# Seven block products for eight in the output and down projections of a two-block transformer kernel

## The reference

```python
xn = rms_norm(h, mix_norm[l])
proj = jnp.einsum("bsd,dp->bsp", xn, w_in[l]) + b_in[l]
...
merged = (jax.nn.sigmoid(ga) * jnp.einsum("bsc,cd->bsd", attn, w_attn_branch[l])
          + jax.nn.sigmoid(gc) * jnp.einsum("bsc,cd->bsd", conv, w_conv_branch[l]))
h = h + jnp.einsum("bsd,de->bse", merged, w_out[l])
hn = rms_norm(h, ffn_norm[l])
up = causal_depthwise_conv(jnp.einsum("bsd,df->bsf", hn, w_up[l]), ffn_conv_w[l])
gate, val = jnp.split(up, 2, axis=-1)
h = h + jnp.einsum("bsf,fd->bsd", jax.nn.silu(gate) * val, w_down[l])
return rms_norm(h, final_norm)
```

## Time and profile before

| | |
|---|---|
| median of 3 runs | 1052.56 us (1052.18 to 1054.4) |
| span of the profiled execution | 1050.5 us, 2.1 below the median |
| TensorE busy | 1038.4 us, 99% of the span |
| VectorE busy | 593.9 us, 57% |
| ScalarE busy | 445.9 us, 42% |
| GpSimd busy | 51.0 us, 5% |
| weight loads by SP, 512 KB each | 150, 3.5 us from issue to landing |

### The profile page before, as it was taken

How to read it: one execution, slowest core, us unless ns; L and a number is a source line. 1 busy time by engine, 2 the same in 40 slices (tenths; PEclk the granted TensorE clock), 3 DMA queues, 4 the chain that set the end, 5 groups by cost and what they waited for, 6 DMA issues and landing times.

```text
span 1050.5 us, 13952 instructions
## 1 busy us (share of the span) xinstructions
PE 1038.4 (99%) x5453; PEld 846.1 (81%) x5453; DVE 593.9 (57%) x1110; ACT 445.9 (42%) x855; POOL 51.0 (5%) x71
## 2 busy tenths in 40 slices
PE   9999999999999999999999999999999999999997
PEld 7877778888888888888888888899888677777785
DVE  6466665445356666533466563553456673567757
ACT  5355542233345434431234442453244454556640
POOL 0000000000001100000000000125200001000000
PEclk9999999999999999999999999999999999999999
DMA  7421133222341842333122323334211222511012
GB/s 277 160 65 57 61 101 100 95 89 98 123 140 41 275 152 87 98 125 110 61 101 85 100 97 110 131 122 135 91 61 61 61 81 71 211 41 41 21 61 80
DMA packets 29106, 107.08 MB, mean 102 GB/s; under 512 B 3227, under 2 KB 3371, under 8 KB 28401
## 3 DMA queue, kind: packets, MB, share of 16 engines
q1 hardware_dynamic: 24864, 86.13, 24.8%
q0 software_dynamic: 4032, 19.96, 5.3%
q10 hardware_dynamic: 144, 0.10, 0.0%
HBM read 101.44 MB, written 7.36 MB: 104 GB/s over the span
## 4 chain that ended last, share of the span: by engine, by line
PE 88%; DVE 5%; ACT 4%; issue 2%; DMA 2%; DVEq 0%; SPq 0%; ACTq 0%
PE ps L780 26%; PE ps L782 25%; PE ps L781 25%; PE ps L1054 2%; PE ps L1222 2%; PE ps L1205 1%; PE ps L1187 1%; DMA raw<-wp 1%; ACT whi L1285 1%; PE ps L1143 1%; PE ps L1106 1%; ACT SC L1336 1%; PE ps L1175 1%; DVE wlo L1633 0%; DVE SC L1739 0%
## 5 line engine op out<-in xcount | busy, mean ns | idle before, releaser
L780 PE MATMUL ps<-XH,whi 128*128 128x512 f32 (+1 forms) x864 | 336.7, 390 | 0.6 <-DVE XL L1646 0.2
L782 PE MATMUL ps<-XH,wlo 128*128 128x512 f32 (+1 forms) x864 | 326.9, 378 | 0.0
L781 PE MATMUL ps<-XL,whi 128*128 128x512 f32 (+1 forms) x864 | 326.5, 378 | 0.0
L1633 DVE TENSOR_TENSOR wlo<-raw,whi 128x1024 fp32r<-128x1024 f32 (+1 forms) x158 | 191.6, 1218 | 166.7 <-ACT whi L1285 166.1
L1285 ACT CAST whi<-raw 128x1024 fp32r<-128x1024 f32 (+1 forms) x158 | 161.2, 1027 | 95.9 <-PE ps L782 70.5
L780 PEld LDWEIGHTS ps<-XH,whi 128*128 128x128 f32 x864 | 162.6, 188 | 43.0 <-issue 12.4
L782 PEld LDWEIGHTS ps<-XH,wlo 128*128 128x128 f32 x864 | 162.6, 188 | 31.2
L781 PEld LDWEIGHTS ps<-XL,whi 128*128 128x128 f32 x864 | 162.8, 188 | 27.8 <-issue 0.5
L780 PE MATMUL ps<-whi,GH 128*128 128x512 f32 x176 | 68.8, 391 | 0.0
L782 PE MATMUL ps<-whi,GL 128*128 128x512 f32 x176 | 68.5, 389 | 0.0
L781 PE MATMUL ps<-wlo,GH 128*128 128x512 f32 x176 | 68.5, 389 | 0.0
(11 more groups left out here) (305 smaller groups left out, 1333.1 us busy)
## 6 DMA issues: line engine op xcount, KB each, us to landing
raw<-wp SPq DMA_DIRECT2D x150, 512.0 KB, 3.5
vec_dram<-row_dram POOLq DMA_DIRECT2D x1, 3072.0 KB, 13.7
H<-x POOLq DMA_DIRECT2D x1, 2048.0 KB, 8.1
x_dram<-H POOLq DMA_DIRECT2D x1, 2048.0 KB, 8.8
A<-w1c POOLq DMA_DIRECT2D x2, 1024.0 KB, 6.3
A<-x_dram POOLq DMA_DIRECT2D x1, 2048.0 KB, 12.8
y<-A SPq DMA_DIRECT2D x8, 256.0 KB, 2.0
raw<-wp SPq DMA_DIRECT2D x4, 402.0 KB, 3.9
```

The costliest lines, as they stand in the source:

```text
L780: self.e.matmul(o, ah, bh, start=start, stop=False)
L781: self.e.matmul(o, ah, bl, start=False, stop=False)
L782: return self.e.matmul(o, al, bh, start=False, stop=stop)
L1633: self.e.tensor_tensor(wlo[BUF[i]][:, 0:w], raw[i % NR][:, 0:w], whi[BUF[i]][:, 0:w].bitcast(F), ALU.subtract).then_inc(sems["lo"], 1)
```

## The change

Each of the two projections is made of 2 x 2 blocks: tokens in two halves, features in pairs of 128-tiles (one of the pair in each half), columns in two halves. Seven products of sums of blocks take the place of the eight products of blocks. `wout` is one group (G = 0, four feature pairs); the FFN is cut into three groups of 8, 8 and 6 up tiles instead of two halves (four, four and three pairs).

- **Products.** `wino(G, p, r)` makes product p for row tile r of a half: all pairs, `mm3` each, 512 columns. Its result, read from PSUM, is added to or subtracted from one or two quarters of H (`INTO`). Two products in a row of the chain may share a bank and add up there. The table `OPERAND` names the sum of features that each uses, in the order in which the products are made.
- **Sums of features** (`sums_of`, `whole`, `summed`): four 256-wide additions per pair on VectorE, and seven 256-wide operands per pair, high parts cast on ScalarE, low parts on VectorE (before four, as whole tiles).
- **Sums of weights.** Products 0, 3 and 4 use blocks as they are, loaded by SP. For products 1, 2, 5 and 6 GpSimd's queue loads blocks and adds others onto them with accumulating DMAs (`add_x`, `add_y`, `wino_sums`) into buffers X and Y.
- **Norm.** `group_normed` puts the norm's steps, and the splits of the next stage's first weights, between products 4, 5 and 6. Squares are taken after products 3 to 6 of the first and the last group.
- **Around it**: banks for the transposes (`NORM_BANKS`); buffers of split parts, five in turn; the bias table's copies after up tile 3 instead of 10; the gain loads earlier; the square root's table loaded ahead of the last merge.

```diff
+OPERAND = [0, 4, 5, 1, 6, 3, 2]
+WBANKS = [(6, 7), (3, 0), (6, 7), (4, 5), (3, 0), (6, 7), (4, 5)]
+INTO = [(0, 0), (1, 1), (0, 1), (0, 0), (0, 1), (1, 1), (1, 0)]
...
-NORM_BANKS = [(4, 5), (3, 0), (4, 5), (3, 6)]
+NORM_BANKS = [(3, 0), (6, 7), (6, 7), (3, 4)]
...
-    def rows_normed(m, rows):
-        for t in range(3):
-            rows(t)
-            if t == 2:
-                en.turn(m, 0)
-            en.norm_rest(m, t)
+    def product(G, p):
+        u = unit(G, p, 0)
+        en.split_all(u + 4)
+        en.wino(G, p, 0)
+        en.split_all(u + 5)
+        en.wino(G, p, 1)
+    def group(G):
+        product(G, 0)
+        product(G, 1)
+        en.wino_sums(G, 2)
+        product(G, 2)
+        en.wino_sums(G, 3)
+        product(G, 3)
+    def group_normed(G, m):
+        group(G)
+        product(G, 4)
+        u = unit(G, 6, 0)
+        en.split_all(u + 2)
+        en.eps_on(m, 0)
+        en.eps_on(m, 1)
+        en.wino(G, 5, 0)
+        en.norm_rest(m, 0)
+        en.wino(G, 5, 1)
+        en.norm_rest(m, 1)
+        en.eps_on(m, 2)
+        en.eps_on(m, 3)
+        en.split_all(u + 4)
+        en.wino(G, 6, 0)
+        en.turn(m, 0)
         en.turn(m, 1)
-        rows(3)
+        en.split_all(u + 5)
+        en.wino(G, 6, 1)
+        en.norm_rest(m, 2)
         en.norm_rest(m, 3)
-        en.turn(m, 2)
...
-    en.begin_norm(1)
-    for c in range(2):
-        for g in range(4 if c == 0 else 2):
-            slot(SLOT_WOUT + 4 * c + g)
-            if c == 1 and g == 1:
-                en.split_all(SLOT_FFN + 2)
-            for t in range(4):
-                en.wout(c, g, t)
-    en.split_all(SLOT_FFN + 3)
-    rows_normed(1, lambda t: en.wout(1, 3, t))
+    for part in range(2):
+        en.merge_sums(3, part)
+    group_normed(0, 1)
 
     en.ffn()
-    for half in range(2):
-        for j in range(11):
-            if half == 0 and j == 0:
-                first_three(1, SLOT_FFN, en.up, [(0, 0, 0, 2), (0, 0, 1, 2), (0, 1, 0, 2)])
+    for G in (1, 2, 3):
+        last = FIRST_F[G] + TILES_OF[G] - 1
+        for f in range(FIRST_F[G], last + 1):
+            if f == last - 2:
+                en.wino_sums(G, 0)
+                en.wino_sums(G, 1)
+            if f == 0:
+                first_three(1, SLOT_FFN, en.up, [(0, 0, 2), (0, 1, 2), (1, 0, 2)])
                 en.distances()
             else:
-                for g in range(1 if half == 0 and j == 1 else 0, 2):
-                    slot(SLOT_FFN + half * N_HALF + 2 * j + g)
-                    en.up(half, j, g, 0)
-                    en.up(half, j, g, 1)
-            en.glu(half, j)
-            if half == 0 and j == 10:
+                for g in range(1 if f == 1 else 0, 2):
+                    slot(up_slot(f, g))
+                    if f == last and g == 1:
+                        en.split_all(unit(G, 1, 1) + 1)
+                    en.up(f, g, 0)
+                    en.up(f, g, 1)
+                    if g == 0 and f % 2 == 0 and f > FIRST_F[G]:
+                        for part in range(2):
+                            en.glu_sums(f // 2 - 1, part)
+            if f == NF - 1:
+                en.begin_norm(2)
+            en.glu(f)
+            if f == 3:
                 en.biases()
-        if half == 1:
-            en.begin_norm(2)
-        for c in range(2):
-            for g in range(6 if half == 0 or c == 0 else 3):
-                i = SLOT_FFN + half * N_HALF + 22 + 6 * c + g
-                slot(i)
-                if half == 1 and c == 1:
-                    en.split_all(i + (4, 5, 7)[g])
-                for t in range(4):
-                    en.down(half, c, g, t)
-    rows_normed(2, lambda t: en.down(1, 1, 5, t))
+        for part in range(2):
+            en.glu_sums(last // 2, part)
+        if G < LAST_G:
+            group(G)
+            for p in range(4, 7):
+                product(G, p)
+        else:
+            group_normed(G, 2)
...
 class Tensor(Engine):
+            def wino(self, G, p, r):
+                t, n = WBANKS[p][r], OPERAND[p]
+                W = GW if G else MW
+                if p == 0:
+                    self.wait_ge("res", added(G - 1, 5, r))
+                    self.wait_ge("tt", 32)
+                    self.wait_ge("cp", 16)
+                elif p == 3:
+                    self.wait_ge("res", added(G - 1, 6, r))
+                elif p == 1:
+                    if G == 0:
+                        self.wait_ge("bm", 16)
+                        self.wait_ge("rsc", SCALED_GATE + 16)
+                    else:
+                        self.wait_ge("ub", 4 * (FIRST_F[G] + TILES_OF[G]))
+                        self.wait_ge("ve", 1)
+                    self.wait_ge("res", added(G - 1, 4, r))
+                else:
+                    self.wait_ge("res", added(G, {2: 0, 4: 1, 5: 2, 6: 3}[p], r))
+                at = 16 + 2 * FIRST_F[G] if G else 0
+                ts = slice(r * P, (r + 1) * P)
+                for s in range(2):
+                    i = unit(G, p, s)
+                    self.wait_ge("hi", i + 2)
+                    self.wait_ge("lo", i + 2)
+                    for m in range(2 * s, min(2 * s + 2, PAIRS[G])):
+                        self.wait_ge("gl", at + 4 * m + (1, 3, 4, 2, 4, 3, 2)[p])
+                        ws = slice((m % 2) * 512, (m % 2) * 512 + 512)
+                        f = self.mm3(ps[t][:, :], W[:, n, 0, m, ts], W[:, n, 1, m, ts], whi[BUF[i]][:, ws],
+                                     wlo[BUF[i]][:, ws], p in (0, 1, 3, 6) and m == 0, m == PAIRS[G] - 1, True)
+                    if r:
+                        f.then_inc(sems["used"], 1)
+                if r == 0:
+                    f.then_inc(sems["tm"], 1)
...
 class Scalar(Engine):
+            def wino(self, G, p, r):
+                if G in (0, LAST_G) and p in (3, 4, 5, 6):
+                    half, c = INTO[p]
+                    self.wait_ge("res", added(G, p, r))
+                    if G == 0:
+                        self.wait_ge("gl", 16)
+                    else:
+                        self.wait_ge("gl", 60)
+                    self.square(2 if G else 1, 2 * half + r, c, p in (4, 6), (UA if G else GA)[:, 0, 0, :])
...
 class Vector(Engine):
+            def wino(self, G, p, r):
+                half, c = INTO[p]
+                h = H[:, 2 * half + r, c * 512:c * 512 + 512]
+                if r:
+                    self.wait_ge("used", unit(G, p, 1) + 1)
+                else:
+                    self.wait_ge("tm", 3 + 7 * G + p + 1)
+                self.wait_ge("xn", 16)
+                back, q = BEFORE[p]
+                self.wait_ge("res", added(G - back, q, r))
+                if p in (2, 5):
+                    self.e.tensor_tensor(h, h, ps[WBANKS[p][r]][:, :], ALU.subtract).then_inc(sems["res"], 1)
+                else:
+                    self.e.tensor_tensor(h, ps[WBANKS[p][r]][:, :], h, ALU.add).then_inc(sems["res"], 1)
+                if p == 5:
+                    h = H[:, 2 + r, 0:512]
+                    self.wait_ge("res", added(G - 1, 6, r))
+                    self.e.tensor_tensor(h, ps[WBANKS[p][r]][:, :], h, ALU.add).then_inc(sems["res"], 1)
...
+            def sums_of(self, X, parity, at):
+                (a11, a21), (a12, a22) = ((X[:, i, 0, 0:256], X[:, i, 0, 256:512]) for i in range(2))
+                s3, s1 = X[:, 0, 1, 0:256], X[:, 0, 1, 256:512]
+                s2, s4 = X[:, 1, 1, 0:256], X[:, 1, 1, 256:512]
+                self.wait_ge("gl", at)
+                if parity == 0:
+                    self.e.tensor_tensor(s3, a11, a21, ALU.subtract).then_inc(sems["ms"], 1)
+                else:
+                    self.e.tensor_tensor(s1, a21, a22, ALU.subtract).then_inc(sems["ms"], 1)
+                    self.wait_ge("ms", at + 2)
+                    self.e.tensor_tensor(s2, s1, a11, ALU.subtract).then_inc(sems["ms"], 1)
+                    self.wait_ge("ms", at + 3)
+                    self.e.tensor_tensor(s4, a12, s2, ALU.add).then_inc(sems["ms"], 1)
+            def whole(self, X, parity, W, m):
+                x = X[:, parity, 0, :]
+                if parity == 0:
+                    self.e.tensor_tensor(W[:, 0, 1, m, :], x[:, 0:256], W[:, 0, 0, m, :].bitcast(F),
+                                         ALU.subtract).then_inc(sems["gl"], 1)
+                else:
+                    self.e.tensor_tensor(W[:, 1:3, 1, m, :], x.rearrange("p (a t) -> p a t", a=2),
+                                         W[:, 1:3, 0, m, :].bitcast(F), ALU.subtract).then_inc(sems["gl"], 1)
+            def summed(self, X, part, W, m):
+                x, n = X[:, part, 1, :].rearrange("p (a t) -> p a t", a=2), 3 + 2 * part
+                self.e.tensor_tensor(W[:, n:n + 2, 1, m, :], x, W[:, n:n + 2, 0, m, :].bitcast(F),
+                                     ALU.subtract).then_inc(sems["gl"], 1)
...
 class Gpsimd(Engine):
+            def add_x(self, G, k, s, n):
+                w = WIDTH[unit(G, 0, s)]
```

(44 more changed lines are left out.)

429 lines of the change are left out of this document (255 added, 174 removed).

## The result

The changed kernel takes **1069.33 us** (median of 4 runs, 1068.53 to 1071.0). The kernel before takes 1053.24 us beside it (4 runs, 1052.18 to 1054.4). The ratio is 1.0154, 95% interval 1.014 to 1.0169: slower by 16.1 us, where 1052.6 was forecast and 1060 was the upper end. The profiled spans say the same, 1066.9 against 1050.5.

A forecast was written before the change was run, and what follows sets the result against it. TensorE was taken as the bound: -20.4 us for matmuls, +18.7 net for norm waits, +1.7 for group starts sum to 0.0 on the 1050.5 us span; with a 2.1 offset, 1052.6. Forecast range 1049 to 1056, outer range 1041 to 1060.

The forecast's parts named there:

- TensorE is the bound and almost gapless: Gate tiles to FFN end: TensorE waits 0.8 us in all, so removed matmuls and new waits count in full.
- Matmuls removed: Both projections, wout and down: 90 fewer matmuls at 0.2265 us each, -20.4 us.
- The ring: Products 3 and 4, first and last group: add, square, cast, low split take 3.6 us a half; TensorE needs 2.7 (2.0 last).
- The chain of 14.4 us from x to the third XL: Product 5 to next stage: serial adds, norm steps, splits and casts; TensorE loses 8.3 us in the first norm, 11.7 last.
- x: Product 5's first residual add, counted from TensorE's ideal end of product 5: 1.1 us in the first group, 3.1 last.
- The lock: VectorE's low splits beside GpSimd's norm products: nothing added; upper end four splits 0.4 us late.
- Starts of the groups: Product 1 waits for the last pair's sums: 0.9 us first group, nothing in groups 1 and 2, 0.8 last; +1.7.
- DMAs: Weight loads: an accumulating load lands in 3.6 us (bounds 3.6 and 10.9), hidden under other work; nothing added.
- rival 3: Product 1 of the first group: slow accumulating loads make it 5 us late at 10.9 us a load, so 1058; chance 0.13.
- Rival 4: Both norms: pauses drop TensorE's clock, the 48 256-column matmuls behind cost 2 to 3 us more each, 1058; chance 0.08.
- Rival 1: Products 3 and 4: the ring keeps up, adds on time, norm losses 4.7 and 6.8 us, so 1044; chance 0.27.

The follow-up runs named there:

- experiment 2: Changed kernel with the squares of product 3 taken one product later and those of product 4 behind product 5's splits: 1055.83 us, ratio 1.0022.
- experiment 1: Changed kernel with every accumulating load made a plain load of the same 512 KB, sums of weight blocks left out: 1055.59 us, ratio 1.0024.
- experiment 5: Changed kernel with 10, 12 and 2 small unread matmuls filling TensorE's pauses in both norms: 1067.69 us, ratio 1.013.
- experiment 7: Changed kernel with accumulating loads made plain and the squares of products 3 and 4 taken later: 1046.58 us, ratio 0.9929.
- experiment 3: Changed kernel with the next stage's two weight splits moved from before product 6 to behind product 4's: 1070.22 us, ratio 1.0164.
- experiment 11: Changed kernel, squares of products 3 and 4 later, X's adding loads behind product 4's casts in groups 1 and 2 alone: 1053.58 us, ratio 1.0001.

## Why the prediction was wrong, step by step

**TensorE is the bound and almost gapless: right**, and so was the rule drawn from it, that each new wait is paid in full. The table's sum shows it within 0.5 us.

**Matmuls removed, -20.4: right.** 90 fewer.

**The ring: right as a mechanism.** 3.55 to 3.8 us a half for 3.6; experiment 2, which takes it away, gains 13.5 us. But the step began its clock at adds that it took to be on time for product 3. Product 5's first add was forecast 1.1 and 3.1 us behind the ideal end of product 5 and came 5.3 and 8.7 behind. With plain loads it came 1.9 and 4.6 behind.

**The chain of 14.4 us from x to the third XL: right**, 14.1. So the losses of 8.3 and 11.7 us are right for their x: experiment 1 shows 8.9 and 13.0.

**The lock.** Low splits beside GpSimd's product took 1.46 and 1.48 us for 1.22 in the first norm, 1.49 for 1.22 and 1.35 for 0.69 in the last: 1.4 us in all, where I had named four splits 0.4 us late as the upper end and taken nothing. A term mis-sized by 1.4 us. The Trainium skill, "SBUF — State Buffer", Who interferes with whom, has the two exclude one another. The rows show the delay, each time 0.13 to 0.15 us shorter than what was left of GpSimd's product when the split began.

**Starts of the groups, +1.7.** The last group's was right (0.7 for 0.8). The first group's was 4.7 for 0.9; with plain loads it is 1.9, so 2.8 us of it belong to the DMA step.

**DMAs, nothing: this is the step that failed.** The text bounded an accumulating load by 3.6 and 10.9 us, took 3.6, "the row of the same size", and priced it at one place, product 1 of the first group; there the loss was 3.8 above forecast, near the 5 us of its other end. That was rival 3. Two things were not in any case. It checked the landing of each accumulating load against its own user, and not what such loads do to the raw loads beside them: 10.0 us to landing for 7.2 with plain loads. "DMA engines are 0.33 busy" was a mean over 70 us of the kernel before; in the 23 us of products 1 to 4 of the first group they are 0.86 busy. And "All other chains have three products (16 us) of cover or more" left out that the ring has no slack to absorb a late weight: a late load shifts the ring, and the ring hands it on whole to the next stage. Of the 16.1 us by which the table's sum exceeds the forecast's, experiment 1 takes away 13.3 (37.8 less 24.5); in time it is 13.7 us.

**Rival 4, the clock: its condition came true, its price didn't, in this kernel.** The clock fell in both norms, and experiment 5 shows in the last that holding it up changes the chain by 0.01 us. The 256-column matmuls behind the norm already ran at 2.4 GHz. That is a matter of timing, not of a low price: other versions, where the clock fell at another time or VectorE's chain is shorter, do pay it. It is 1.3 to 1.5 us behind a norm in experiments 5 and 7, an estimated 3.4 in experiment 3, and 2.9 in product 1 of the first group in experiment 11.

**Rival 1** was a good account of the kernel without the loads' cost: 1044 forecast for adds on time, 1046.6 measured in experiment 7.

## What to carry to other kernels

Count a DMA that adds into its target as two, on the engines and not only at its user, and look at the busy share of the DMA engines in the very stretch where the new loads fall. Then ask for each transfer beside them which weight it feeds and how much slack the queue behind it has: a ring of engines that runs slower than the bound passes every delay on, so break the ring first (here two squares moved back in ScalarE's queue were worth 13.5 us). A granted clock that falls inside a wait costs nothing as long as the slowed work still ends before what it waits for. Look again in every new version: each wait that is removed leaves less to hide it, and here it came to 2.9 us in a version that only drew level with the kernel before.

## What the runs showed of the hardware

- A 512 KB load from GpSimd's queue that accumulates takes 8.1 us at the median to land (X, 4.8 to 15.3), 5.3 as a plain load in the same places (3.8 to 9.9). Of the 16 engines' time it costs some 2.8 us for 1.5.
- With accumulating loads under way the 16 engines, 0.86 busy, moved 203 GB/s; with plain ones 232 GB/s at 0.67 busy (39.7 + 26.8 + 0.3%).
- GpSimd takes 0.86 us to issue an accumulating load of X and 0.53 for a plain one in its place.
- TensorE fell from 2.4 to 1.2 GHz behind or in pauses of 1.6 to 2.9 us a few microseconds apart, at 323.0 and 691.6 us, and was back at 2.4 after 6.8 and 10.2 us, both times while it still worked through the end of the group. At the low level 512-column matmuls come 0.43 us apart instead of 0.23, and 3.4 us of it in gapless work cost 1.5 to 1.6 us (experiments 5 and 7).
